# Moving q/k products, a gate tile and half of the output projection inside one layer of a streaming encoder

## The reference, cut to what matters

```
proj = rmsnorm(x) @ w_in                  # 2048 columns: u, xm, v, o_pre, 512 each
y_a  = s5_group(u)                        # 32 groups: B.u, complex diagonal scan over time, C.state + D.u,
                                          # g = gelu(y);  g * sigmoid(g @ w_glu)
xc   = silu(causal_conv4(xm))             # 4 heads of 128
q, k = xc @ w_q, xc @ w_k                 # per head
gates = concat(q, k, v) @ w_gates + b     # 8 rows: input and forget gates
h    = mlstm_chunkwise(q, k, v, gates)    # 4 heads, computed as decay-weighted attention over 512 positions
y_b  = sigmoid(o_pre) * rmsnorm(h)
x    = x + concat(y_a, y_b) @ w_out
```

## Time and profile before

| | |
|---|---|
| median of the runs | 1131.56 us |
| profiled execution | 1132.59 us, span 1130.8 us |
| TensorE busy | 1094.9 us, 5542 instructions |
| VectorE, ScalarE, GpSimd busy | 649.8, 465.2, 208.8 us |
| mean granted TensorE clock | 0.990 |
| HBM traffic | 106.73 MB, 94 GB/s |

### The profile page before, as it was taken

How to read it: one execution, slowest core, us unless ns; L and a number is a source line. 1 busy time by engine, 2 the same in 40 slices (tenths; PEclk the granted TensorE clock), 3 DMA queues, 4 the chain that set the end, 5 groups by cost and what they waited for, 6 DMA issues and landing times.

```text
span 1130.8 us, 15508 instructions
## 1 busy us (share of the span) xinstructions
PE 1094.9 (97%) x5542; PEld 883.0 (78%) x5542; DVE 649.8 (57%) x871; ACT 465.2 (41%) x671; POOL 208.8 (18%) x312
## 2 busy tenths in 40 slices
PE   9969998999999999999999999999999999999997
PEld 7847656887888888888887777777888888888886
DVE  6798863556666666653333666266666666652323
ACT  6424553445434443432323365355434444432221
POOL 7998991020000000000000022030000000000000
PEclk9989998999999999999999999999999999999999
DMA  6641200422232222232333211032322223323222
GB/s 218 167 97 60 91 1 1 167 94 94 93 101 103 93 93 93 96 109 98 107 107 116 68 56 57 21 129 94 106 98 93 93 94 103 99 93 112 94 93 75
DMA packets 36491, 106.73 MB, mean 94 GB/s; under 512 B 7840, under 2 KB 10144, under 8 KB 36320
## 3 DMA queue, kind: packets, MB, share of 16 engines
q1 hardware_dynamic: 36448, 106.15, 28.7%
HBM read 101.55 MB, written 3.15 MB: 93 GB/s over the span
## 4 chain that ended last, share of the span: by engine, by line
PE 82%; DVE 4%; ACT 3%; issue 2%; POOL 0%; DVEq 0%; ACTq 0%; POOLq 0%
PE bank L1401 25%; PE bank L1403 25%; PE bank L1402 25%; PE bank L1743 1%; PE bank L1424 1%; ACT whi L645 1%; PE bank L1765 1%; PE bank L1563 1%; DVE h L1217 1%; PE bank L1596 0%; ACT sq L651 0%; PE bank L1543 0%; DVE xlo L949 0%; DVE wlo L943 0%; POOL ssum L435 0%
## 5 line engine op out<-in xcount | busy, mean ns | idle before, releaser
L1401 PE MATMUL bank<-xhi,whi 128*128 128x512 f32 x992 | 391.4, 395 | 7.6 <-DVE xlo L949 2.9
L1402 PE MATMUL bank<-xlo,whi 128*128 128x512 f32 x992 | 386.7, 390 | 0.0
L1403 PE MATMUL bank<-xhi,wlo 128*128 128x512 f32 x992 | 386.6, 390 | 0.0
L943 DVE TENSOR_TENSOR wlo<-raw,whi 128x1024 fp32r<-128x1024 f32 x177 | 223.5, 1263 | 269.0 <-ACT whi L645 268.4
L645 ACT ACTIVATE whi<-raw 128x1024 fp32r<-128x1024 f32 x177 | 187.1, 1058 | 378.3 <-PE bank L1403 350.6
L1401 PEld LDWEIGHTS bank<-xhi,whi 128*128 128x128 f32 x992 | 186.6, 188 | 52.1 <-issue 6.1
L1403 PEld LDWEIGHTS bank<-xhi,wlo 128*128 128x128 f32 x992 | 186.5, 188 | 39.4
L1402 PEld LDWEIGHTS bank<-xlo,whi 128*128 128x128 f32 x992 | 186.6, 188 | 38.6 <-issue 1.0
L1401 PE MATMUL bank<-ahi,whi 128*128 128x512 f32 (+1 forms) x374 | 142.5, 381 | 0.0
L1403 PE MATMUL bank<-ahi,wlo 128*128 128x512 f32 (+1 forms) x374 | 141.6, 379 | 0.0
L1402 PE MATMUL bank<-alo,whi 128*128 128x512 f32 (+1 forms) x374 | 140.4, 375 | 0.0
(11 more groups left out here) (236 smaller groups left out, 1097.4 us busy)
## 6 DMA issues: line engine op xcount, KB each, us to landing
raw<-wstream SPq DMA_DIRECT2D x177, 512.0 KB, 3.3
xin<-xT SPq DMA_DIRECT2D x8, 256.0 KB, 6.1
raw<-wstream SPq DMA_DIRECT2D x8, 256.0 KB, 5.3
h<-xT SPq DMA_DIRECT2D x1, 2048.0 KB, 8.4
outT<-outb SPq DMA_DIRECT2D x8, 256.0 KB, 2.2
u_scratch<-uperm SPq DMA_DIRECT2D x1, 1024.0 KB, 5.6
uc<-u_scratch SPq DMA_DIRECT2D x8, 128.0 KB, 5.2
bcp<-bc SPq DMA_DIRECT2D x1, 512.0 KB, 4.6
```

The lines of the kernel that those rows point to most:

```text
L943: V.tensor_tensor(wlo[:, t % RING, :], raw[:, t % RAWS, :], whi[:, t % RING, :].bitcast(f32), ALU.subtract).then_inc(lo_done, 1)
L1401: MM(dst, wh, rhi, start=start, stop=False)
L1402: MM(dst, wh, rlo, start=False, stop=False)
L1403: return MM(dst, wl, rhi, start=False, stop=stop)
```

## The change

Seven edits, one new order:

1. TensorE: q/k products, gate tile 13 and the gate sums now stand ahead of the `gre`/`gim` transposes and the small products. The `vtok` transposes come directly behind the `xs` copies.
2. ScalarE: copies `cdiag` (VectorE did) and both q and k (VectorE did q); behind these come the hi splits of tiles 16 and 17, and then the `m1re`/`m1im` copies, which used to stand ahead of them. GpSimd clears `cdiag` at the start.
3. VectorE: evacuations of projections 9, 10 and 11 without splits and `g_step`s between them; then lo split of tile 13, three `g_step`s, `g8`, lo splits 14, 15, 16, the first gate tile, lo split 17, and read-outs 0 to 4.
4. Operands in PSUM: the conv accumulates in bank 7 instead of `cacc`; `g_step` reads its factors from a copy in bank 4 and writes one of two intermediate results to bank 5. The gate sums go to bank 7.
5. Memory: `qT`/`kT` get places of their own; `m1re`/`m1im` go where `vtok` will be; `g8` moves.
6. TensorE: 12 of the 16 blocks of the heads' half (the three first heads), and the last mean square, ahead of the S5 outputs; the four blocks of the last head behind the half-GLU. Both sets of S5 transposes come ahead of the whole half-GLU and use banks 4 and 5.
7. ScalarE: the gelu table is loaded earlier, the last head's hi copy ahead of the first gelu.

```diff
 # TensorE
         for t in range(RING, 12):
             project(t, t)
+        pe.wait_ge(lo_done, T_QK + 1)
+        pe.wait_ge(xclo_done, HEADS)
+        for b in range(8):
+            hd = b % 4
+            if b < 4:
+                pe.wait_ge(out_freed, max(k + 1 for k in range(12) if IN_BANK[k] == QK_BANK[hd]))
+            else:
+                pe.wait_ge(q_evac, hd + 1)
+            block3(bank[QK_BANK[hd]][:, :], T_QK % RING, b, xchi[:, hd, :], xclo[:, hd, :], True,
+                   True).then_inc(qk_ready, 1)
+        pe.wait_ge(k_evac, 1)
+        project(T_O, O_O)
+        pe.wait_ge(k_evac, HEADS)
+        pe.wait_ge(rms_done, 1)
+        for k in range(12):
+            q = k % 4
+            ins = MM(bank[7][32 * q:32 * q + 8, :], cols("wg")[:, 8 * k:8 * k + 8],
+                     (qT, kT, vT)[k % 3][:, k // 3, :], start=k < 4, stop=k >= 8)
+        ins.then_inc(gates_ready, 1)
         pe.wait_ge(g_built, CH - 4)
         pe.wait_ge(g_mid, 3)
         for b in range(8):
+            if b == 3:
+                pe.wait_ge(gates_copied, 1)
             if b >= 4:
                 pe.wait_ge(m1_copied, b - 3)
...
+        pe.wait_ge(lo_done, T_YB + 2)
+        pe.wait_ge(e_done, SB * HEADS)
+        for b in range(4, 6):
+            pe.wait_ge(yb_done, b - 3)
+            yb_block(b, 2)
+        mean_square(HEADS - 1)
+        pe.wait_ge(num_gated, HEADS)
+        pe.wait_ge(dsq_done, HEADS)
+        for b in range(4, 6):
+            for m in range(2):
+                yb_block(b, m)
+        pe.wait_ge(yb_done, 3)
+        for m in range(3):
+            yb_block(6, m)
+        pe.wait_ge(hms_added, HEADS)
+        for b in range(4, 7):
+            yb_block(b, 3)
         pe.wait_ge(toep_built, 16 * CH)
         pe.wait_ge(scan_done, 1)
...
         s5_output(0)
         s5_output(1)
-        mean_square(HEADS - 1)
         s5_output(2)
-        pe.wait_ge(hms_added, HEADS)
         s5_transposes(0)
         s5_output(3)
+        s5_transposes(1)
 # (the half-GLU in one piece, then)
+        pe.wait_ge(yb_done, 4)
+        for m in range(4):
+            yb_block(KB - 1, m)
 # ScalarE
+        for f in range(2):
+            r = slice(STATE * f, STATE * f + STATE)
+            A(cdiag[r, :, :, f, :], bcp[r, 2:4, :].rearrange("p r (j i) -> p r j i", i=GCH),
+              ACT.Copy).then_inc(cdiag_set, 1)
+        for hd in range(HEADS):
+            act.wait_ge(qk_ready, hd + 1)
+            A(qT[:, hd, :], bank[QK_BANK[hd]][:, :], ACT.Copy).then_inc(q_evac, 1)
+        for hd in range(HEADS):
+            act.wait_ge(qk_ready, HEADS + hd + 1)
+            A(kT[:, hd, :], bank[QK_BANK[hd]][:, :], ACT.Copy).then_inc(k_evac, 1)
+        split_hi(T_QK + RING)
+        split_hi(T_O + RING)
         for b in range(8):
             act.wait_ge(m1_ready, b + 1)
 # VectorE
         for t in range(12):
+            wait_tile_used(dve, max(t, 3))
+            if 0 < t < 9:
                 split_lo(t + RING)
...
+        dve.wait_ge(g0_done, 1)
+        dve.wait_ge(q_done, 1)
+        split_lo(T_QK + 1)
+        dve.wait_ge(out_freed, 7)
+        steps.up(V.tensor_copy(qp, qq[:, :, :, :]))
         settle()
+        for step in range(1, 4):
+            g_step(step)
+        dve.wait_ge(gates_ready, 1)
+        V.tensor_scalar(g8[:, :], bank[7][0:104, :], col("bgate", 0, 104), None, ALU.add).then_inc(gates_copied, 1)
+        split_lo(T_QK + 2)
+        split_lo(T_QK + 3)
+        wait_tile_used(dve, T_QK)
+        split_lo(T_QK + RING)
+        out_gate(0)
         for step in range(3):
             read_out(step)
```

More of the change, by code:

```diff
@@ L189, in build @@
     F4 = [P, 2, PAIRS, P]
-    (ff, gg, m1re, m1im, uc, uperm, xchi, xclo, sigo, xs, ksb) = plan(
-        ("ff", F4, f32), ("gg", F4, f32), ("m1re", F2, f32), ("m1im", F2, f32),
+    (ff, gg, qT, kT, uc, uperm, xchi, xclo, sigo, xs, ksb) = plan(
+        ("ff", F4, f32), ("gg", F4, f32), ("qT", [P, HEADS, SEQ], f32), ("kT", [P, HEADS, SEQ], f32),
         ("uc", [P, GROUPS, NCH], f32), ("uperm", [P, 4, SEQ], f32),
@@ L200, in build @@
     toep = at("toep", [P, CH, GROUPS, GCH], gg_at)
[L201 removed]
+    gtmp = at("gtmp", [P, 2, PAIRS, GCH], base)
     gsig = at("gsig", [P, 4, SEQ], base)
     xin = at("xin", [P, KB, SEQ], m1_at)
[L204 to L205 removed]
+    m1re = at("m1re", F2, xc_at)
+    m1im = at("m1im", F2, xc_at + 8192)
     ga = at("ga", [P, 4, SEQ], m1_at)
@@ L420, in _ @@
         G.memset(xpad[:, 0:3], 0.0)
+        G.memset(cdiag[:, :, :, :, :], 0.0)
         G.memset(xs[:, :, :, 0:1], 0.0).then_inc(pads_set, 1)
@@ L1004, in read_out, with out_gate @@
             dve.wait_ge(f_done, s + 1)
+        def out_gate(m):
+            wait_tile_used(dve, T_O + m)
+            V.tensor_tensor(sigo[:, m, :], bank[IN_BANK[O_O + m]][:, :], rstd[:, :], ALU.mult).then_inc(out_freed, 1)
+            if m < 3:
+                split_lo(T_O + m + RING)
         def conv_lo(m):
@@ L1030, in _ @@
                     dve.wait_ge(xcf_done, m)
[L1031 to L1032 removed]
+                else:
+                    dve.wait_ge(rms_done, 1)
+                acc = bank[7][:, :]
+                steps.up(V.tensor_scalar(acc, xpad[:, 3:], col("mlw", 4 * m + 3), col("mlb", m), ALU.mult, ALU.add))
                 for w in (2, 1, 0):
                     settle()
[L1035 to L1037 removed]
+                    ins = V.scalar_tensor_tensor(out=acc, in0=xpad[:, w:w + SEQ], scalar=col("mlw", 4 * m + w),
+                                                 in1=acc, op0=ALU.mult, op1=ALU.add)
                     if w:
@@ L1472, in _ @@
             ins.then_inc(s5in_ready, 1)
-        pe.wait_ge(lo_done, T_QK + 1)
-        pe.wait_ge(xclo_done, HEADS)
-        for b in range(8):
-            o = O_QK + b % 4
-            if b < 4:
-                pe.wait_ge(out_freed, max(k + 1 for k in range(o) if IN_BANK[k] == IN_BANK[o]))
-            else:
-                pe.wait_ge(out_freed, o + 1)
-            block3(bank[IN_BANK[o]][:, :], T_QK % RING, b, xchi[:, b % 4, :], xclo[:, b % 4, :], True,
-                   True).then_inc(qk_ready, 1)
-        pe.wait_ge(k_evac, 1)
-        project(T_O, O_O)
-        pe.wait_ge(s5in_copied, 2)
-        pe.wait_ge(k_evac, HEADS)
-        for k in range(12):
-            q = k % 4
-            ins = MM(bank[4][32 * q:32 * q + 8, :], cols("wg")[:, 8 * k:8 * k + 8],
-                     (qT, kT, vT)[k % 3][:, k // 3, :], start=k < 4, stop=k >= 8)
-        ins.then_inc(gates_ready, 1)
+        pe.wait_ge(s5in_copied, 2)
         for hd in range(HEADS):
@@ L1606, in _, with yb_block @@
         broadcast_floor(HEADS - 1)
+        def yb_block(b, m):
+            ins = block3(bank[m][:, :], (T_YB + m // 2) % RING, 4 * (m % 2) + b - 4, xhi[:, b, :],
+                         xlo[:, b, :], b == 4, False)
+            if b == KB - 1 and m % 2:
+                ins.then_inc(tile_used, 1)
+        pe.wait_ge(lo_done, T_YB + 2)
[15 more added lines that the diff above has]
+            yb_block(b, 3)
         pe.wait_ge(toep_built, 16 * CH)
```

104 lines of the change are left out of this document (27 added, 77 removed).

## The result

| | before | after |
|---|---|---|
| median of the runs | 1131.84 us (1131.46 to 1132.54, 4 runs) | 1144.9 us (1143.45 to 1146.35, 4 runs) |
| ratio | | 1.0115, interval 1.0097 to 1.0132 |
| profiled execution | 1132.59 us, span 1130.8 | 1144.19 us, span 1142.4 |
| mean granted clock | 0.990 | 0.988 |

Slower, as forecast, but by 13.1 us instead of 6.3; 1144.9 lies outside the range of 1132 to 1143. The two profiled executions are 11.6 us apart.

The account below looks back on a forecast made before the run. TensorE, busy over 97% of the span, was taken as the bound. Terms +2.35 (front), +1.5 (mean square), -4.2 (S5 outputs to half-GLU) and +6.7 (before the S5 half) gave +6.3: 1137.9 us, range 1132 to 1143.

Parts of the forecast that it names:

- end point: Moment the output projection's first four columns are done: 227.8 us before, 234.1 forecast; later delays count one for one.
- q to k wait: TensorE between q and k products, waiting for ScalarE's first q copy from 76.4 to 82.4: 6.0 us, bounds 5.3 to 7.
- Cold start behind it: the first mis-sized term: k products after the q to k wait run at the low clock for 3.2 us: +1.5 us, bounds 0 to 1.9.
- The split chain in front of `m1re`: S5 input transposes wait for `m1re` behind hi splits 16 and 17, 97.2 to 103.15: 6.0 us, 5 to 8.
- Heads "the same work with the same waits": From `vtok` to the heads' end nothing changes; heads end at 174.78 + 2.35 = 177.1 us.
- Mean square and moved blocks: Between heads and S5 outputs: 9.1 us of work plus 1.5 around the mean square, from 177.1 to 187.7.
- The scan: GpSimd's scan starts at 113.5 after the `xs` copies, ends at 184.5 to 188.3, just hidden by the moved blocks.
- the scan decides: Rival: a full 74.8 us scan and late inputs put S5 outputs from 191, +10 us, 1142; chance 0.12.
- S5 outputs to half-GLU: From the first S5 output at 187.6 to the half-GLU at 202.8: 15.2 us, a -4.2 us term.
- Split 21: TensorE waits before the S5 half for VectorE's lo split of tile 21, behind the gating: 5.2 us, 4 to 6.
- Cold start behind it: the second mis-sized term: After the split 21 wait, matmuls run at the low clock: +1.5 us, bounds 0 to 1.9.
- PSUM operands: Conv accumulator and `g_step` operands in PSUM: nothing faster, 0.1 x 4 us more in the conv, hidden; 0.4 if uncovered.

Follow-up runs that it names:

- where the read-outs met the scan: The changed kernel with ScalarE's hi splits of tiles 16 and 17 behind the `m1re` and `xs` copies: 1152.55 us, ratio 1.0186.
- the kernel with the changed back alone: The kernel before, with the changed kernel's order from the end of the heads on: 1138.95 us, ratio 1.0059.

## Why the prediction was right in direction and wrong in size

The places were right: every long wait stands where it was forecast, with the releaser named. The sum was 6.3 us, and the profiled executions are 11.6 apart; at the end point they are so already (227.96 and 239.59). Step by step:

- **q to k wait.** 6.0 predicted, 5.59 measured; k from 82.4 predicted, 82.23 measured.
- **Cold start behind it: the first mis-sized term.** I took +1.5, "3.2 us at 1.2 GHz", from the earlier trace rows and the 2.6 us at 193. From 82.23 to 88.32 there are 14 matmuls in 6.09 us, where 14 x 0.227 = 3.2: +2.9. The gate sums ended at 96.1, not 94.9: 1.2 us of the error. The bound of 1.9 was too low too. By the times of the run with unread matmuls the cold clock of the two front waits is worth 3.3 to 3.7 us.
- **The split chain in front of `m1re`: right in kind, 1 us short.** TensorE was to go on at 103.15 and did at 105.34; 1.2 of this came from the gate sums, and tile 17 landed 4.3 us behind the end of its split (99.4 to 103.74) instead of 3.4, before which ScalarE stood idle for 1.14 us. From there to `vtok` it took 10.4 us, as forecast. `vtok` began 4.58 us later than before, not 2.35. That this step carries the change is shown: undoing it alone (lo splits 14 and 15 early) gave back 9.6 us.
- **Heads "the same work with the same waits": wrong by 1.5 us.** They ended 6.06 us later than before, 180.84 against 174.78, though they began 4.58 later. From the first `vtok` transpose to the last weighted sum it was 62.4 us before and 63.7 after; in the other kernels it was 62.5 to 62.8 with the old front and 63.6 to 65.8 with the new (83.0 where the read-outs met the scan; the 65.4 to 65.8 among them are executions whose clock fell behind the 2.17 us wait). The difference is in TensorE's waits, 4.8 us in all instead of 3.5. At 152.46 it waits 1.69 for VectorE's `wbuf`, 0.97 at that place before. Ahead of that `wbuf` VectorE does a read-out product in 1.23 us, 0.68 before, and GpSimd's scan beside it works on 128x256 where it had come to 128x32 before. So the likely cause is VectorE beside a scan that runs later; no run isolates it.
- **Mean square and moved blocks.** 10.6 predicted (187.7 - 177.1), 10.63 measured (191.47 - 180.84), the cold end of the heads included.
- **The scan.** Start 113.5 and end 184.5 to 188.3 predicted; 115.86 and 187.0 measured. The rival "the scan decides" fell for the changed kernel, and is true of it without the moved blocks.
- **S5 outputs to half-GLU.** 15.2 predicted, 15.50 measured.
- **Split 21.** Wait of 5.2 predicted, 5.13 measured; 18.8 from the half-GLU to the end of the wait predicted, 18.98 measured. Taking it away gave 4.2 us.
- **Cold start behind it: the second mis-sized term.** +1.5 predicted; 13 matmuls from 225.95 to 231.65 took 5.70 instead of 2.95: +2.75, 1.25 us of the error.

In all 1.2 + 1.0 + 1.5 + 0.3 + 0.2 + 1.25 = 5.45, less 0.15 because the end point before was 227.96 and not 227.8: 5.3, which makes 11.6 of the 6.3. The other 1.5 us between 11.6 and 13.1 is that the profiled execution after is 0.7 below its median and that of before 0.75 above its own. **The step that failed** is the price of a cold start, +1.5 each time where the two measured +2.9 and +2.75: I read it from one execution and bounded it at 1.9. Its length is not fixed by the wait in front of it. Behind the q to k wait (5.35 to 6.80 us) the seven profiled executions that have it without unread matmuls show 9 to 14 cold matmuls, +2.0 to +2.9; behind the 5.1 us wait six show 8 to 13, +1.7 to +2.8; and behind the 12.6 us wait, where I had read 3 to 4 us at 1.2 GHz, the kernel with the changed back alone has 5.8. That the changed kernel's profiled execution is at the long end of both is in part chance; that +1.5 was too little is not. The second miss is the unchanged stretch of heads, which I did not bound at all.

The Trainium skill ("TensorE: Matmul & The Clock Gate", Part 1, "What's actually happening") has it that activity lifts the clock. The run with unread matmuls agrees: 1.00 where it was 0.50, and the kernel with 54 more instructions is the faster one.

**PSUM operands.** That they are worth nothing here was right for the changed kernel (1145.03 against 1144.9). The reason I gave was not whole: I compared 589 ns in SBUF with 680 for an evacuation. The first conv instruction does take longer in PSUM at 43 us, 0.81 against 0.55, so for it the rule that the prediction quotes holds. That nothing is faster in PSUM does not hold. It depends on what GpSimd does meanwhile: at 43 us GpSimd, busy with operands of 128x32, slows none of the conv in SBUF; at 64 us, beside its products of 128x512, the same first instruction takes 1.28 instead of 0.55 and the three steps 3.72 instead of 2.35, while in PSUM they stay at 0.80 and 2.34. A rule that I had not weighed bears on this: the Trainium skill ("SBUF — State Buffer", "SBUF: two separate sides") has it that a GpSimd operation and a VectorE operation in a mode of two ports, or one with two SBUF inputs (this against a GpSimd operation that reads SBUF), lock each other out of a shared port pair. The trace agrees for the products with two tensors (0.69 with one in PSUM, 1.22 and 1.54 without). Its "exclusive lock" for a whole instruction is neither shown nor excluded: the slowed operations took 0.5 to 0.9 us more, while GpSimd's beside them lasted 1.07 to 1.7.

## What to carry to other kernels

When TensorE work is moved, follow not only its operands but the prefetch behind it: here each weight split that stood behind a wait for TensorE cost a transfer, a copy and a cold start, and moving two lines of VectorE's program gave back 9.6 of 13.1 us. Charge a cold start per wait of some us with a range from several executions, up to the longest cold stretch that a trace shows. Ask also what now comes later than it did: here the S5 inputs, and with them the scan. Test the parts of a bundled change apart: the one that I had at nothing was worth 0.7% in the old order and nothing in the new, and without that test the new order looks 8 us better than it is.

## What the runs showed that I had not expected

- Cold stretches differ from execution to execution at one and the same wait: 3.5 to 5.7 us behind the wait of 5.1, 4.0 to 6.1 behind that from q to k. The wait of 2.17 us for `xs` left the clock up in four profiled executions and down in four (the selecting products behind it take 1.88 or 3.57 us).
- Work that nobody reads, put into a wait, makes the kernel faster: 1144.9 to 1141.16 us by the medians, with intervals of the ratios that just meet.
- VectorE beside GpSimd operations of 128x512: three conv steps take 3.72 us in SBUF and 2.34 with the accumulator in PSUM; beside GpSimd operations of 128x32 they take 2.35 in SBUF. A read-out of four operations takes 2.2 us before the scan and 3.9 beside it.
